# Prompt and decode hybrid layer: page gathers, gate buffer, engine orders, last head's loads, and the compression layer as three rounded products

## The reference

```python
def compress_blocks(x, pe, w1, w2):              # x (B, L, 2 groups, 64)
    blocks = x[:, idx] + pe[:, None, :]          # windows of 32 tokens, one every 16
    flat = blocks.transpose(0, 1, 3, 2, 4).reshape(B, n_cmp, G, 32 * 64)
    return jax.nn.silu(flat @ w1) @ w2           # w1 (2048, 128), w2 (128, 64)

kc = compress_blocks(k_cmp, pk_pe, pk_w1, pk_w2) # and the same for the values;
                                                 # 63 windows of the prompt, 31 of each sequence
log_a = (jax.nn.log_sigmoid((a_low @ a_up + a_b)) / GLA_GATE_TAU)
b = jnp.cumsum(gc, axis=2)                       # gc: log_a in chunks of 32 tokens
q_dec, k_inv, k_tail = qc * jnp.exp(b), kc * jnp.exp(-b), kc * jnp.exp(b_last - b)
S = jnp.exp(bl[:, 0])[..., None] * S + jnp.einsum('bjhd,bjhv->bhdv', kt, vv)
mix = jax.nn.sigmoid(g_a) * (o_nsa @ w_ba) + jax.nn.sigmoid(g_b) * (o_g @ w_bb)
y = x + mix @ w_out
```

## Time and profile before

| | us |
|---|---|
| median of 3 runs (1449.09 to 1455.34) | 1452.5 |
| the profiled execution, whole | 1457.85 |
| its span, first to last instruction | 1456.0 |
| PE busy in the span | 1359.3 (93%) |
| ACT, DVE, POOL busy | 635.2, 571.5, 140.5 |
| mean granted TensorE clock | 0.970 |

### The profile page before, as it was taken

How to read it: one execution, slowest core, us unless ns; L and a number is a source line. 1 busy time by engine, 2 the same in 40 slices (tenths; PEclk the granted TensorE clock), 3 DMA queues, 4 the chain that set the end, 5 groups by cost and what they waited for, 6 DMA issues and landing times. The chain is left out here.

```text
span 1456.0 us, 23589 instructions
## 1 busy us (share of the span) xinstructions
PE 1359.3 (93%) x9565; PEld 1191.5 (82%) x9565; DVE 571.5 (39%) x1229; ACT 635.2 (44%) x1086; POOL 140.5 (10%) x170
## 2 busy tenths in 40 slices
PE   4999999999999999999999999998768868899998
PEld 4999899998978888888888888886455658899876
DVE  5211122315623434344333323332588645553332
ACT  5212234412333557655675568554647532221111
POOL 2100011003201000000000000011700170000000
PEclk9999999999999999999999999999789979999999
DMA  8431362312222112221122112112653645444231
GB/s 207 139 91 44 105 134 82 110 36 65 59 60 54 47 53 60 74 59 56 58 76 58 59 55 74 45 46 62 223 174 128 210 144 156 147 135 114 91 109 68
DMA packets 141242, 137.19 MB, mean 94 GB/s; under 512 B 27088, under 2 KB 125728, under 8 KB 141072
## 3 DMA queue, kind: packets, MB, share of 16 engines
q1 hardware_dynamic: 138352, 127.27, 29.0%
q0 software_dynamic: 2784, 8.43, 2.0%
HBM read 97.82 MB, written 41.88 MB: 96 GB/s over the span
## 5 line engine op out<-in xcount | busy, mean ns | idle before, releaser
L217 PE MATMUL ps<-hH,wH 128*128 128x352 f32 (+1 forms) x1320 | 445.1, 337 | 5.6 <-DVE hL L489 3.3
L217 PE MATMUL ps<-hH,wL 128*128 128x352 f32 (+1 forms) x1320 | 426.4, 323 | 0.0
L217 PE MATMUL ps<-hL,wH 128*128 128x352 f32 (+1 forms) x1320 | 426.1, 323 | 0.0
L217 PEld LDWEIGHTS ps<-hH,wH 128*128 128x128 f32 (+1 forms) x1320 | 248.4, 188 | 48.6 <-issue 37.8
L217 PEld LDWEIGHTS ps<-hL,wH 128*128 128x128 f32 (+1 forms) x1320 | 249.3, 189 | 2.8 <-issue 1.9
L217 PEld LDWEIGHTS ps<-hH,wL 128*128 128x128 f32 (+1 forms) x1320 | 248.4, 188 | 0.9
L1206 DVE CUSTOM_DVE_ANT_0 sP<-ps,dist 128x128 f32<-128x128 f32 (+3 forms) x128 | 57.7, 489 | 233.8 <-PE ps L1031 233.8
L1269 ACT ACTIVATE pPT<-ps 128x512 f32<-128x512 f32 (+3 forms) x104 | 49.1, 472 | 196.6 <-PE ps L1045 196.3
L204 DVE TENSOR_TENSOR wL<-w_raw,wH 128x1024 fp32r<-128x1024 f32 (+1 forms) x55 | 66.9, 1216 | 160.9 <-ACT wH L196 160.9
L303 ACT ACTIVATE stg<-ps 128x352 f32<-128x352 f32 x132 | 60.9, 462 | 83.0 <-PE ps L217 76.6
L1310 ACT ACTIVATE sP<-sP,stat 128x640 f32<-128x640 f32 (+7 forms) x128 | 93.2, 730 | 2.9 <-DVE stat L1206 2.2
(11 more groups left out here) (335 smaller groups left out, 2058.8 us busy)
## 6 DMA issues: line engine op xcount, KB each, us to landing
w_raw<-in_w_in SPq DMA_DIRECT2D x46, 512.0 KB, 4.1
p_spill<-stg SPq DMA_DIRECT2D x132, 176.0 KB, 1.8
zt<-p_spill SPq DMA_DIRECT2D x24, 528.0 KB, 4.9
gvT<-p_spill SPq DMA_DIRECT2D x8, 528.0 KB, 5.9
rq<-p_spill SPq DMA_DIRECT2D x8, 528.0 KB, 4.7
x_all<-in_x_prompt SPq DMA_DIRECT2D x8, 512.0 KB, 10.2
w_raw<-in_w_in SPq DMA_DIRECT2D x16, 256.0 KB, 3.9
S<-in_state_gla SPq DMA_DIRECT2D x4, 1024.0 KB, 5.5
```

The source lines that it names most:

```text
L217: mm = nc.tensor.matmul(ps[0:t.m, bank, 0:NF], w[:, c % 2, t.m * k:t.m * k + t.m], x[:, k, NF * n:NF * n + NF], start=(k == 0 and i == 0), ...
```

## The change

**Compression.** `hidden` becomes three rounded products like the rest. `w1` is split into `w1H` (ACT) and `w1L` (DVE), the gathered tokens lie in one array for prompt and sequences (`xr`, 12 rows; high part `xH`, rest `xL`), and one product covers 384 columns at steps 0 and 2, 256 at steps 1 and 3. The position term is summed on DVE (`bias_rows`, 16 linked instructions) and needs one one-column product. The first split of `w1` stands in block 1. The array has no second half, so all copying for the next step waits for `hidden` of this one. To make room `w_raw` has two buffers and `pages` four. PE's order is changed so that a unit stands between `turn` and `hidden`.

**Decode.** POOL gathers the first values already in block 3, ahead of the keys, and both wait for the last unit. `zl` of head 1 has a buffer of its own; `gates(2)`, `gates_out(2)`, `log1p`, `exps` and the DVE steps are put elsewhere; `sums(1)` and `tails(1)` go to the start of block 5, and `inputs(0)` behind the first masks.

**Last head.** `m_raw`'s first tile is loaded before the states of head 2 are stored; ACT's `o_high` moves two steps back, and both `high` and both `low` of the ring behind the last state.

```diff
-        raw = at("w_raw", [P, 3, KT * P], RING)
+        raw = at("w_raw", [P, 2, KT * P], RING)
-        NPG = 5
+        NPG = 4
...
+        def w1_high(act, kv):
+            act.wait_ge(sem("w1_loaded"), 16 * (kv + 1))
+            for j in range(2):
+                nc.scalar.activation(w1H[j][:, :, :], w1[:, 8 * j:8 * j + 8, :], ACT.Copy).then_inc(sem("w1_high"), 1)
+        def bias_rows(dve, link, kv):
...
+            for s in range(16):
+                col = pe2[:, kv, s:s + 1]
...
+                    ins = nc.vector.scalar_tensor_tensor(out=bsumw[:, :], in0=w1[:, s, :], scalar=col, in1=bsumw[:, :],
+                                                         op0=ALU.mult, op1=ALU.add)
+                link(ins)
...
                 def hidden(st):
...
+                    first = 0 if half == 0 else 4
                     for s in range(16):
...
+                        for i, (w, x) in enumerate(((wH, xH), (wH, xL), (wL, xH))):
+                            mm = nc.tensor.matmul(ps[:, 0, 32 * first:32 * NX].rearrange("p (n c) -> p n c", c=32), w,
+                                                  x[:, first:NX, c0:c0 + 32], start=(s == 0 and i == 0),
+                                                  stop=(s == 15 and i == 2))
...
                 turn(0)
+                pe_units(pe)
+                hidden(0)
                 turn(1)
                 pe_units(pe)
-                hidden(0)
+                hidden(1)
+                pe_units(pe)
+                second(0)
                 turn(2)
-                pe_units(pe)
-                hidden(1)
-                pe_units(pe, 2)
-                second(0)
+                pe_units(pe, 3)
+                hidden(2)
                 turn(3)
...
+                def batches(st):
+                    if st >= 1:
+                        act.wait_ge(sem("hid_done"), st)
+                    for n in range(NB * st, NB * st + NB):
+                        page_of(copy, act, 1, n, "act")
+                        if n % 2 == 1:
+                            act.wait_ge(sem("cX_dve"), n + 1)
+                            act.wait_ge(sem("cX_act"), n + 1)
+                            copy(pair(xH, n // 2), pair(xr, n // 2)).then_inc(sem("cX_high"), 1)
+                            act_units(act)
...
-                pool.wait_ge(sem("w_low"), NT)
-                fetch_pages(pool, 0, "k", raw[:, :, :].rearrange("p n c -> p (n c)")[:, 0:NB * 512].rearrange(
-                    "p (b c) -> p b c", b=NB))
+                pool.wait_ge(sem("u_done"), NU)
+                fetch_pages(pool, 0, "v", vp[:, 0, :, :])
+                fetch_pages(pool, 0, "k", raw[:, :, :].rearrange("p n (b c) -> p (n b) c", c=512))
                 add(4 * R - 1)
...
-        zl = at("zl", [P, TOK], 83008)
+        zls = [at("zl0", [P, TOK], 83008), at("zl1", [P, TOK], 146496)]
...
-                pe.wait_ge(sem("zl_copied"), 2)
-                gates(pe, 2)
+                    elif u == 3:
+                        pe.wait_ge(sem("zl_copied"), 2)
+                        gates(pe, 2)
...
-                fetch_pages(pool, 0, "v", vp[:, 0, :, :])
                 fetch_pages(pool, 2, "k", kp[0][:, :, :])
...
+                sums(dve, 1)
+                tail_sums(0)
+                tails(dve, link, 1)
...
-                    if not next1:
-                        mring.low(dve, 0)
                     state(h, 6)
...
                     sample(h)
+                    if not next1:
+                        mring.low(dve, 0)
+                        mring.low(dve, 1)
...
+                    if h + 2 == GH:
+                        sp.wait_ge(sem("su_done"), h + 1)
+                        mring.load(sp, 0)
                     for b in range(0, DB, 2):
```

More of the change, by code:

```diff
@@ L220, in products @@
                 return mm
-        ring = Ring(tiles, raw, wH, wL, 3, FIRST)
+        ring = Ring(tiles, raw, wH, wL, 2, FIRST)
         qT = at("qT", [P, R, TOK], REST)
@@ L254, in hybrid_step @@
         w1 = at("w1", [P, 16, P], REST + 43008)
+        w1L = at("w1L", [P, 16, P], REST + 43008, FR)
+        w1H = [at("w1Ha", [P, 8, P], RING + 8192, FR), at("w1Hb", [P, 8, P], REST + 96288, FR)]
+        bsumw = at("bsumw", [P, P], REST + 79040)
+        ones = small[:, 56:57]
         def load_w1(eng, kv):
@@ L531, in _ @@
                 dve.wait_ge(sem("vectors"), 16 * 6)
-                dve_units(dve, 9)
+                link(nc.vector.memset(ones, 1.0))
+                dve_units(dve, 5)
+                bias_rows(dve, link, 0)
+                w1_low(dve, 0)
+                dve_units(dve, 4)
             @block.scalar
@@ new lines, in page_of @@
+            def page_of(copy, eng, par, n, name):
+                eng.wait_ge(sem("pT_done"), n + 1)
+                for g in range(G):
+                    ins = copy(xr[HD * par:HD * par + HD, 4 + NB * g + n % NB, :].rearrange(
+                                   "p (j s c) -> p j c s", j=2, s=4)[:, :, 0:32],
+                               ps[HD * g:HD * g + HD, turn_bank(n, par), 0:2 * P].rearrange(
+                                   "p (j c s) -> p j c s", j=2, s=4))
+                ins.then_inc(sem("cX_" + name), 1)
@@ L1883, in _ @@
                 queries(dve, link, 0)
+                keys(dve, link, 0)
+                minus_abs(dve, 1)
                 copy_probs(4)
                 score(5)
+                inverses(dve, 0)
                 output(4)
-                log_sigmoid(dve, link, 1)
-                copy_probs(5)
-                sums(dve, 1)
-                output(5)
-                inverses(dve, 0)
                 spans(dve, link, 0)
@@ L1894, in _ @@
                     dve.wait_ge(sem(f"p_stored{n}"), 16 * ((NU - n + NSTG - 1) // NSTG))
+                copy_probs(5)
                 later_queries(link, 0)
-                tails(dve, link, 1)
+                output(5)
+                log_sigmoid(dve, link, 1)
             @block.scalar
@@ L1922, in _ @@
                 turned(act, 0, 3)
-                exps(act, 0)
+                log1p(act, 0)
                 probs(3)
@@ L2228, in _ @@
                     masked(h, 1)
+                    if h == 0:
+                        inputs(0)
                     if next1:
```

223 lines of the change are left out of this document (127 added, 96 removed).

## The result

The changed kernel takes 1441.4 us (median of 4 runs, 1440.8 to 1442.0) where the kernel before takes 1453.9; the ratio is 0.9919, with an interval from 0.9892 to 0.9945. The forecast was 1421, with a range that ended at 1436. So the direction was right, but of 31 us only some 13 came. The profiled execution has a span of 1440.1 us.

What follows compares the result with a forecast made beforehand. PE bounds block 2; block 4 and the end of the heads are relays of engines waiting for each other. 16.5 + 8 + 6.8 = 31.3 us off the 1452.5 median gives 1421, range 1410 to 1436.

Steps and rivals of the forecast that it cites:

- the one that moved the gathers: End of block 3: eight gathers behind the last unit land by 1012, before block 4, removing PE's 4.15 us wait.
- Compression, PE: Block 2, four `hidden` steps: rounded products cut PE's 45.5 us to 28.8, saving 16.7.
- The line through products of 352 and 512 columns: Block 2 product price: 0.44 ns a column and 7 ns fixed, so 176 ns for 384 columns, 120 for 256.
- Compression, feeders: Block 2, ACT and DVE feeding PE: about 2 us wait in step 1, 0.2 us allowed; compression net 16.5 us.
- Block 4: Decode block: earlier gathers and reordered ACT and DVE work end it about 9 us earlier, net 8 us.
- The walk: Order traced through block 4: value products of pass 2 start 7 us earlier, the block takes 51 us.
- Block 5, heads 0 to 2: Start of block 5: `sums(1)` and `tails(1)` ahead of the first mask cost head 0 1 us.
- Last head: Head 3: splits behind the last state let the samples' products start at 1172.6, not 1179.4; 6.8 us saved.
- (a): Block 4 and the last head: ACT holds PE as the values did, gain 22.5 us in all, 1430; chance 0.12.
- (b): Block 2: compression is fed too late, each step's copying exposed, so it brings 7 us; 1431 in all; chance 0.10.
- (d): Block 2: rounded products read short strided runs slowly, 1.64 ns a column, 55 us lost, 1493 in all; chance 0.03.
- (c): Block 4 and last head: denser order keeps the array at full clock, some 6 us more gain, 1415; chance 0.09.

Runs made afterwards that it cites:

- decode_only: The kernel before with the decode part alone, compression and last head as before; 1459.6 us, ratio 1.0034.
- k_early: The changed kernel with keys gathered first and earlier, only the values behind the last unit: two bursts of four gathers, not eight; 1429.4 us, ratio 0.9835.
- aligned: The changed kernel with column offsets of `hidden` rounded down to multiples of 4 (16 bytes), so wrong tokens are read; 1424.7 us, ratio 0.9812.
- decode_shift1: The kernel before with the decode part alone, shifted by 1 us through 8 repeated transpose products; 1452.2 us, ratio 0.9983.
- v_block4: The changed kernel with the values gathered in block 4 again, the keys still in block 3; 1431.3 us, ratio 0.9851.
- after_again: The changed kernel run once more, unaltered; 1440.6 us, ratio 0.9905 to the kernel before.
- comp_only: The kernel before with the compression part alone, decode and last head as before; 1442.0 us, ratio 0.9911.
- head_only: The kernel before with the last head's part alone; 1448.3 us, ratio 0.9956.
- k_early_shift1: The changed kernel with two bursts of four gathers (keys early), shifted by 1 us through 8 more products; 1429.9 us, ratio 0.9844.
- k_early_aligned: The changed kernel with keys gathered early and column offsets of `hidden` rounded down to multiples of 4 (wrong tokens); 1427.3 us, ratio 0.9808.

## Why the prediction was wrong

**The missing stage.** The step that failed is the one that moved the gathers: they "now run in block 3", and the sum had no term for what block 3 pays for it. Block 3 was taken as fixed, without a reason. I had worked out when the gathers are done and land (landed by 1012 of before, a microsecond ahead of the block), and that was right: the packets end at 996.4, block 4 starts at 1005.0. What the runs showed in its place is that updates by PE came up to 4.3 us late beside the gathers, and ACT, DVE and then PE stood for them; with half clock around it this cost 5 us at the end of block 3 (6 in decode_only). The other 1.9 of the 6.7 us are left of the half clock at its start. Between profiles, 31.3 us were forecast and 15.9 came. Of the 15.4 missing, block 3 has 6.7, block 4 5.4 (9 forecast, 3.6 came), compression 1.8, heads 0 to 2 1.7 and the last head 0.5; 0.7 came elsewhere.

How much of block 4 is the late update's is less clear. The changed kernel has 56.7 us there. The four kernels that differ from it by a shift alone have 53.9 to 55.0, so 1.7 to 2.8 us go with the late update; the rest to the 51.6 of k_early is in kernels without it too. Three of these four are also 1.6 us longer in head 0, so even that part is not all loss. In the medians the shifts put the whole at 8 to 11 us (1429.8 to 1432.8 against 1440.6). Without that loss the time would lie inside the range, which goes from 1410 to 1436. Why the updates came late, and whether the eight gathers have a part in it, stays open.

**Compression, PE.** Forecast 28.8 us for the four steps, measured 9.34, 6.15, 9.42 and 6.15, together 31.1. The term mis-sized is the product: 176 and 120 ns were about right for 12 of 48 (176 and 117), 195 and 131 are true for 36. The line through products of 352 and 512 columns could not show it, as these read whole rows.

**Compression, feeders.** Right that nothing else holds PE up. PE waits 0.9 and 0.6 us for ACT's copies in step 1 (forecast 2), none for `xL`, `w1L` or `bsumw`, and none for `w_raw` anywhere. Full clock behind the single one-column product, as said. Block 2 won 14.7 us where 16.5 were forecast, and 17.2 in aligned.

**Block 4.** The walk came true in three of the eleven profiles that have the new orders and no late update. `gates(1)` comes 22.1 us into the block in k_early (forecast 23), 27.9 in the changed kernel; the block is 51.6 us in k_early, aligned and decode_shift1 (forecast 51). In the others it is 53.9 to 55.0, and there half clock holds for 10.2 to 17.1 us in one piece around its start, where k_early has two pieces of 3.4. Between kernels with the same code in the block, the 2 to 3 us go with this half clock (v_block4 also has its wait for `vp`); no step of the walk had it, though the earlier trace rows showed a mean clock of 0.76. Nor did the walk have the wait for ACT that took the place of the one for `vp`.

**Block 5, heads 0 to 2.** 1 us was forecast as the cost for head 0, and 0.8 measured, but kernels without the decode part have 28.7 in head 0 too, and six of those with it 29.7 to 29.9, so the traces don't show what the moved scan costs. The 1.7 us more of head 1 are half clock (0.93 of full) and are not there in after_again.

**Last head.** Right, and the reason too: 6.3 us in the first profile and 6.1 in the medians, for 6.8. The state landed 5.7 us after its issue. POOL's splits ended at 1168.2, ahead of PE.

**The rivals.** (a), the relay gives it back, had the symptom right: PE waits for ACT in place of `vp`, 3.75 us for 4.15 in k_early. Its size was wrong, since the same orders give 51.6 us: PE's waits of over 1.5 us in block 4 come to 6.9 us in k_early, 9.7 in the changed kernel and 10.4 in the kernel before. In the changed kernel taken alone, the sign that the prediction had set for this, PE's waits moved to ACT with the same sum, was nearly met. (b) and (d) did not happen, though (d) asked the right question, whether the rounded type reads short runs slower, and priced it at 1.64 ns a column, 0.63 us for a product of 384, where 0.195 us came. (c), the clock, was put on the wrong side only: it took up to 3 us in block 4 and 2.8 at the start of block 3. The Trainium skill, TensorE: Matmul & The Clock Gate (What's actually happening), says that activity releases the throttle; the traces agree, in that the 3 us of idle time between blocks stand ahead of the half clock at 324.3 in the changed kernel, but the same idle time stands at 336.9 in the kernel before and full clock follows, so the rule did not tell me which I would get.

**The base.** The profiled execution of before was 3 to 4 us above the median, and part of what the sum took off was luck of that execution: in the projections it has 270.7 us, and most of the later kernels 267 to 269 with the same work. Without a stall the gain is 22 to 25 us in the medians and 24 to 31 between profiles, so even then it stays under the 31.3 of the sum.

## What to carry to other kernels

Before a change is believed to be slow or fast, time it once more with everything a microsecond later: a shift that adds work and makes the kernel 10 us faster says that the loss hangs on the moment and not on the work that the edit adds or saves. When transfers are gathered into one burst beside engines that pass work to each other, ask not only when they land but what the stage around them may pay, and give it a term in the sum. Splitting the burst was free here, and the three kernels with two bursts of four had no stall; that the split is what spared them is not shown. And let short runs of a rounded operand start on 16 bytes.

## What the runs showed of the hardware

- An update of a semaphore by PE, recorded 0.01 to 0.02 us after the modelled end of its product as a rule, came up to 4.3 us late at the end of block 3 (4.9 in decode_only) and up to 5.2 in block 4 (comp_only); ACT, DVE and in turn PE stood for it. In the changed kernel it repeated in a second execution, with PE's and ACT's idle times the same to 0.02 us, and was gone when everything came 0.5 us later.
- A rounded product reading runs of 32 columns costs 195 ns in place of 176 at 384 columns, and 131 in place of 117 at 256, when its runs start off a multiple of 4 columns.
- Stages with the same instructions differ by 2 to 3 us with the time for which half clock holds in them: block 3 by 2.6 (head_only and the kernel before), block 4 by 2.3 (k_early and k_early_shift1) and 3.1 (aligned and k_early_aligned).
- A gather took POOL 0.94 to 1.00 us, eight times in a row, with DVE's copies and softmax steps beside it; the 2.3 us that the prediction weighed for block 3 did not come.
